# The ring of low weights, and all that is placed behind it, 64 bytes further on

## What is computed

```python
def swiglu(x, w_gu, w_down):
    gate, up = jnp.split(x @ w_gu, 2, axis=-1)
    return (jax.nn.silu(gate) * up) @ w_down
...
for i in range(N_A_LAYERS):
    x = x + 0.5 * swiglu(rms_norm(x, ffn1_norm[l]), ffn1_w_gu[l], ffn1_w_down[l])
    h = rms_norm(x, mix_norm[l]) @ a_w_in[i]
```

## Time and profile before

| | |
|---|---|
| median of 3 runs | 1196.7 us |
| lowest, highest | 1196.52, 1197.67 us |
| profiled execution, first to last instruction | 1195.0 us |
| PE busy | 1187.3 us (99%), 7956 matmuls |
| DVE busy | 934.7 us (78%) |
| ACT busy | 730.4 us (61%) |

### The profile page before, as it was taken

One profiled execution on the slowest core, in us unless ns is written; L12 is line 12 of the kernel. 1 busy time (PEld: TensorE's weight loads), 2 busy tenths in 40 slices (PEclk: granted clock), 3 DMA queues, 4 the chain that ended last, 5 costly groups with the idle time before them and its releaser, 6 DMA issues.

```text
span 1195.0 us, 22393 instructions
## 1 busy us (share of the span) xinstructions
PE 1187.3 (99%) x7956; PEld 1089.4 (91%) x7956; DVE 934.7 (78%) x1617; ACT 730.4 (61%) x1211; POOL 77.9 (7%) x91
## 2 busy tenths in 40 slices
PE   9999999999999999999999999999999999999998
PEld 9899999888888999999888889988888989888887
DVE  7766788988876788688988767888876787888853
ACT  7564746666654588567666645666664567666642
POOL 4460000000000000610000000000000000000000
PEclk9999999999999999999999999999999999999999
DMA  8545655554654445115555743655663423555730
GB/s 329 184 142 187 232 189 177 186 208 176 230 214 154 141 170 188 41 36 177 211 178 204 258 151 123 211 176 194 219 239 135 150 91 125 195 205 178 255 131 36
DMA packets 48143, 209.92 MB, mean 176 GB/s; under 512 B 3486, under 2 KB 4908, under 8 KB 43596
## 3 DMA queue, kind: packets, MB, share of 16 engines
q1 hardware_dynamic: 46720, 204.96, 48.7%
q10 hardware_dynamic: 1356, 4.07, 1.0%
HBM read 207.90 MB, written 1.13 MB: 175 GB/s over the span
## 4 chain that ended last, share of the span: by engine, by line
PE 93%; DVE 4%; ACT 1%; issue 1%; DMA 1%; DVEq 0%; SPq 0%; ACTq 0%
PE main L2165 25%; PE main L2167 13%; PE main L2523 13%; PE main L2138 8%; PE main L2139 8%; PE main L2140 8%; PE main L2525 7%; DVE w_lo L1157 1%; PE side L2303 1%; PE main L2566 1%; PE side L2566 1%; PE side L2277 1%; PE main L2682 1%; PE main L2854 1%; PE main L2858 1%
## 5 line engine op out<-in xcount | busy, mean ns | idle before, releaser
L1157 DVE TENSOR_TENSOR w_lo<-raw,w_hi 128x1024 fp32r<-128x1024 f32 (+3 forms) x365 | 466.8, 1287 | 5.0 <-ACT w_hi L594 3.8
L2165 PE MATMUL main<-xs,w_hi 128*128 128x512 f32 x1328 | 461.3, 390 | 0.2 <-DVE xs L1191 0.2
L594 ACT ACTIVATE w_hi<-raw 128x1024 fp32r<-128x1024 f32 (+2 forms) x363 | 402.5, 1111 | 68.3 <-PE main L2140 53.0
L2167 PE MATMUL main<-xs,w_lo 128*128 128x256 f32 x1328 | 374.5, 282 | 0.0
L2165 PEld LDWEIGHTS main<-xs,w_hi 128*128 128x128 f32 x1328 | 249.2, 188 | 53.2 <-DVE w_lo L1157 0.7
L2167 PEld LDWEIGHTS main<-xs,w_lo 128*128 128x128 f32 x1328 | 251.0, 189 | 0.0
L2523 PE MATMUL main<-h_both,w_hi 128*128 128x512 f32 x682 | 236.6, 390 | 0.0
L2525 PE MATMUL main<-h_both,w_lo 128*128 128x256 f32 x682 | 192.3, 282 | 0.0
L2523 PEld LDWEIGHTS main<-h_both,w_hi 128*128 128x128 f32 x682 | 128.0, 188 | 26.8
L2525 PEld LDWEIGHTS main<-h_both,w_lo 128*128 128x128 f32 x682 | 128.9, 189 | 0.0
L2138 PE MATMUL main<-xs,w_hi 128*128 128x256 f32 x368 | 105.4, 286 | 0.0
(11 more groups left out here) (505 smaller groups left out, 1869.6 us busy)
## 6 DMA issues: line engine op xcount, KB each, us to landing
raw<-in_w_gu_a SPq DMA_DIRECT2D x44, 1024.0 KB, 5.2
raw<-in_w_gu_b SPq DMA_DIRECT2D x44, 1024.0 KB, 5.2
raw<-in_w_down_a SPq DMA_DIRECT2D x16, 1408.0 KB, 6.1
raw<-in_w_down_b SPq DMA_DIRECT2D x16, 1408.0 KB, 6.0
raw<-in_w_in SPq DMA_DIRECT2D x15, 1024.0 KB, 5.4
raw<-in_w_in_a SPq DMA_DIRECT2D x13, 1024.0 KB, 5.2
raw<-in_w_gates SPq DMA_DIRECT2D x4, 1024.0 KB, 5.1
raw<-in_w_up SPq DMA_DIRECT2D x4, 1024.0 KB, 5.2
```

Source lines behind the costliest of these rows:

```text
L594: act.activation(w_hi[:, u % RING, 0:n], raw[:, s % RAW, u % 2, 0:n], ACT.Copy).then_inc(hi_ready, 1)
L1157: return dve.tensor_tensor(dst, src, hi.bitcast(F32), ALU.subtract)
L2165: pe.matmul(bank[:, :], piece(w_hi, u, k), xs[:, k], start=k == 0, stop=k == KC - 1, skip_group_check=True)
L2167: ins = pe.matmul(bank[:, 0:SEQ], piece(w_lo, u, k), xs_hi[:, k], start=False, stop=k == KC - 1, skip_group_check=True)
```

## The change

`w_lo` is placed 64 bytes behind the end of `w_hi` instead of directly behind it, so everything placed after it moves by 64 bytes as well. Behind `h_both` another 96 bytes are left free, so that what is placed after it moves by 160: `gate_n`, `gate_s`, `hid`, `xk_hi`, `xk_lo`, `k_nope`, `k_rope`, `v_mla`, `v_pad_b`, `final`. The views `xs` and `h_both` become one view for each stage, taken from a table of offsets; all offsets in the tables equal the places of before (32 and 0), so nothing is changed by that. No instruction, wait, or transfer is added, removed or moved.

```diff
+XS_AT = {"out1": 32, "ffn_a1": 32, "mix_a": 32, "ffn_a2": 32, "ffn_b1": 32, "mix_b": 32, "ffn_b2": 32}
+H_AT = {"a1": 0, "a2": 0, "b1": 0, "b2": 0}
...
+        def placed(name, at, n):
+
+            e = at % 32 // 4
+            return nc.alloc_sbuf_tensor_at(name, [P, e + n], F32R, offset=at - 4 * e)[:, e:e + n]
+
         x, at = place("x", (nc.sbuf_base + 31) // 32 * 32, [P, KC, SEQ])
-        xs, _ = place("xs", at + 32, [P, KC, 2, SEQ], F32R)
-        xs_hi, xs_lo = xs[:, :, 0], xs[:, :, 1]
+        xs_of = {name: placed("xs_" + name, at + off, KC * 2 * SEQ).rearrange("p (k i n) -> p k i n", k=KC, i=2)
+                 for name, off in XS_AT.items()}
...
         w_hi, at = place("w_hi", at, [P, RING, UNIT], F32R)
-        w_lo, at = place("w_lo", at, [P, RING, UNIT], F32R)
+        w_lo, at = place("w_lo", at + 64, [P, RING, UNIT], F32R)
...
-        h_both, at = place("h_both", free0, [P, 2, FT, SEQ], F32R)
-        h_hi, h_lo = h_both[:, 0], h_both[:, 1]
+        h_of = {name: placed("h_" + name, free0 + off, 2 * FT * SEQ).rearrange("p (i k n) -> p i k n", i=2, k=FT)
+                for name, off in H_AT.items()}
+        at = free0 + 4 * 2 * FT * SEQ + 96
```

More of the change, by code:

```diff
@@ L782, in residual @@
                 if name != "end2":
-                    scale_hi(xs_hi[:, row, :], x[:, row, :], gain("ffn_b1" if name == "kv" else name, row))
+                    split = "ffn_b1" if name == "kv" else name
+                    scale_hi(xs_hi_of[split][:, row, :], x[:, row, :], gain(split, row))
                 square(x[:, row, :], SEQ, c + m)
@@ L823, in up @@
                     act.wait_ge(hid_ready, f * FT + t + 1 + i * 4)
-                    act.activation(h_hi[:, row, :], hid[:, t % 2, :], ACT.Copy).then_inc(h_hi_ready, 1)
+                    act.activation(h_of[which][:, 0, row, :], hid[:, t % 2, :], ACT.Copy).then_inc(h_hi_ready, 1)
                 turns = (FT - first - 2) // 4
@@ L1050, in _ @@
                 act.wait_ge(hid_ready, f * FT + t + 1)
-                act.activation(h_hi[:, t, :], hid[:, t, :], ACT.Copy).then_inc(h_hi_ready, 1)
+                act.activation(h_of["b1"][:, 0, t, :], hid[:, t, :], ACT.Copy).then_inc(h_hi_ready, 1)
                 if t == 0:
@@ L1494, in residual @@
                     dve.wait_ge(evac, t + m + 1 + off)
-                    scale_lo(xs_lo[:, row, :], xm, gain(split, row), xs_hi[:, row, :],
+                    scale_lo(xs_lo_of[split][:, row, :], xm, gain(split, row), xs_hi_of[split][:, row, :],
                              XG0[split] + m, off)
@@ L1552, in hidden @@
                     dve.wait_ge(h_hi_ready, n + 1 + b)
-                    low(h_lo[:, tt, :], hid[:, t % 2, :], h_hi[:, tt, :]).then_inc(h_ready, 1)
+                    low(h_of[which][:, 1, tt, :], hid[:, t % 2, :], h_of[which][:, 0, tt, :]).then_inc(h_ready, 1)
                 turns = (FT - first - 2) // 4
@@ L1846, in _ @@
                 dve.wait_ge(h_hi_ready, f * FT + t + 1)
-                low(h_lo[:, t, :], hid[:, t, :], h_hi[:, t, :]).then_inc(h_ready, 1)
+                low(h_of["b1"][:, 1, t, :], hid[:, t, :], h_of["b1"][:, 0, t, :]).then_inc(h_ready, 1)
                 if t == 0:
@@ L2157, in project, with project_halves @@
                 unit_end(ins)
-            def project_halves(u, bank, off=0, first=None):
+            def project_halves(u, bank, xs, off=0, first=None):
                 unit_begin(u, off)
@@ L2166, in project_halves @@
                               skip_group_check=True)
-                    ins = pe.matmul(bank[:, 0:SEQ], piece(w_lo, u, k), xs_hi[:, k], start=False, stop=k == KC - 1,
+                    ins = pe.matmul(bank[:, 0:SEQ], piece(w_lo, u, k), xs[:, k, 0], start=False, stop=k == KC - 1,
                                     skip_group_check=True)
@@ L2491, in ffn @@
                 f, u0, t0 = FFNS.index(which), first_unit("w_gu_" + which), FIRST_TILE["gu_" + which]
+                xs, h_both = xs_of[FFN_NORM[which]], h_of[which]
                 def turn(i, first=None):
                     if first is not None and which != "a1":
-                        enter(u0, [bank_of(t0 + j) for j in range(2)], (xs_hi, xs_lo) if which == "b2" else (xs,), first,
+                        enter(u0, [bank_of(t0 + j) for j in range(2)], (xs[:, :, 0], xs[:, :, 1]) if which == "b2" else (xs,), first,
                               2 if which == "b2" else 1, None if which == "b2" else FFN_NORM[which])
@@ L2498, in turn @@
                         if which == "b2" and first is not None:
[L2499 removed]
+                            project(u0 + j, bank_of(t0 + j)[:, 0:SEQ], xs[:, :, 0], xs[:, :, 1],
                                     within=(KC - 2, lambda: norm_sum(FFN_NORM[which])) if j == 2 else None)
                         else:
[L2502 removed]
+                            project_halves(u0 + j, bank_of(t0 + j, i * 4), xs, i * 4, first if j == 0 else None)
                         if first is not None and which == "a1" and j == 0:
@@ L2524, in down @@
                                           stop=k == FT - 1, skip_group_check=True)
-                                ins = pe.matmul(bank[:, 0:SEQ], piece(w_lo, u, b), h_hi[:, k, :], start=False,
+                                ins = pe.matmul(bank[:, 0:SEQ], piece(w_lo, u, b), h_both[:, 0, k, :], start=False,
                                                 stop=k == FT - 1, skip_group_check=True)
```

40 lines of the change are left out of this document (22 added, 18 removed).

## The result

The changed kernel takes 1203.96 us, the median of three runs (1203.65 to 1205.06), against 1196.7 before: a ratio of 1.006, 95% interval 1.0042 to 1.0078. It is slower, by 7.3 us. The profiled execution spans 1202.1 us, 7.1 more than the 1195.0 of before.

A forecast was written before the change was run, and what follows sets the result against it. PE, busy 99% of the 1195.0 us span, was taken as the bound. Long matmuls (5.1 us) and short ones (0.7 us) added 5.8 us, giving 1200.8, plus an unchanged 1.7 us around the span: 1202.5 us, range 1188.0 to 1206.5.

The forecast's parts named there:

- The rule that carried it: Likeliest case, slower, chance 0.41: minus 32 is a worse distance than 32 for weights loaded beside the long matmul.
- The long matmuls of the `xs` pairs: 512-column matmuls beside low-weight loads: 1344 at 3.8 ns more each, 5.1 us, the pair going to 350.5 ns.
- The changed short loads: Short matmuls beside a load at a changed distance, in `h_both` pairs and triples: 1814 at 0.4 ns, 0.7 us.
- the choice of the smallest reading: Pricing short matmuls at 0.4 ns, the smallest direct reading at 256 columns, since mixed distances seemed to cost little.
- the small projection: Matmuls passing through eight distances, 117.9 ns on average as on `xs`; taken as evidence against a strong dependence on distance.
- The prices of the 272-column rows: `xg` read from its first token, at minus 32 before the change: 1.1 to 3.3 ns more per matmul.
- The 160 bytes of `xk`: Moved `xk_hi` and `xk_lo`, 72 matmuls: at most 0.7 us at 10 ns each, as likely nothing; only in the range.
- The rival "same": Distance makes no difference or repeats every 64 bytes, so the time stays at 1196.7 us; chance 0.28.
- The rule quoted from the Trainium skill: PE has two independent read ports, so loading weights takes no read bandwidth from the running matmul; time would stay 1196.7 us.
- The rival "faster": Unequal distances to high and low weights break an unlucky rhythm of stream and load: 5 to 8 us gained, 1190 us; chance 0.31.

The follow-up runs named there:

- e1: Changed kernel with the low-weight ring put back directly behind the high one, views by stage and 96 bytes behind `h_both` kept: 1196.78 us.
- e2: Changed kernel with the low-weight ring in its old place and everything behind it still 64 bytes further on: 1200.81 us.
- e7: Changed kernel with `acc` and everything behind it 192 bytes further on, so all tokens are at 32 from high and 224 from low weights: 1204.53 us.
- e11: Changed kernel with low weights directly behind high ones and everything in SBUF, tokens included, 64 bytes further on: 1196.98 us.
- e3: Changed kernel with low weights, and everything behind them, moved by 128 bytes instead of 64: 1199.62 us.
- e6: Changed kernel with other offsets of `xs` and `h_both` in each feed-forward part, low weights still 64 bytes on: 1204.88 us in one execution.
- e12: Changed kernel run again unedited, in five more executions and with a new profile: 1203.97 us.

## Why the prediction was right, and where its steps were off

*Direction and size.* 1202.5 us was forecast, 1203.96 measured, in a range of 1188.0 to 1206.5. The rule that carried it, a distance of minus 32 costs more than one of 32 for the low weights loaded beside the long matmul, is what e1, e2, e7 and e11 show. That the sum came within 1.5 us is in part luck: one term was too high and the other far too low.

*The long matmuls of the `xs` pairs*, 3.8 ns and 5.1 us, measured 4.4 us, 3.3 ns on average over 1328. The forecast was one rate of 350.5 ns; there are two, 348.9 and 353.3, whose mean is near by luck. The price, too, was weaker than it looks: 2.56 us over 11 starts, from rows given to 10 ns, leaves it open by 0.9 ns either way. In b2 the short matmul got longer too (120.6 ns on average against 118.3), which the forecast excluded. So the term is about right and the picture behind it too simple.

*The changed short loads*, 0.4 ns on 1814 matmuls, 0.7 us: off in its parts. In the `h_both` pairs it was 0.0, as the page shows. In triples behind the rings it was 2.2 ns on average, 5 times my price, and over all three matmuls of a triple, not the two with a changed load. `xg` lost 1.0 to 1.1 ns on average, and not where the forecast put it: between 98 and 119 us the first matmul of a triple, the one with the changed load beside it, stayed at 116.0 ns, and the second and third went from 117.0 to 119.2 and 118.1. Together 2.7 us instead of 0.7. The step that failed is the choice of the smallest reading because of the small projection: its 117.9 ns is an average over distances, in which good and bad ones cancel, and it says little on any one of them. The prices of the 272-column rows, 1.1 to 3.3 ns, were the better guide.

*The 160 bytes of `xk`* are next to nothing, as allowed for: at 192/128 its 72 matmuls take 118.1 ns on average, against 117.2 before, 0.1 us.

*The rival "same"* rested on a period of 64 bytes or none. The shift by 64 is the whole effect (e1), and a shift by 128 still shows (e3). The rule quoted from the Trainium skill, "TensorE: Matmul & The Clock Gate", section "Step-by-step: what each phase is for", does not hold for these operands: with the same instructions and clock, where the loaded blocks lie relative to the tokens changes the time by 2.2 or 6.7 ns a pair in the kernel after, and moving both together changes nothing (e11), so loading is not free for the running matmul. What the two streams meet in, no run here shows.

*The rival "faster"* needed a pair below 346.7 ns. For this change it is out: every stage of the kernel after is at 346.7 or above. As an idea it is not. It said that unequal distances can win back part of the 26.7 ns of excess, and at 64/0 in e6 a pair ran at 340.0 ns, an excess of 20.0, until a stall. Even an equal distance, 192/192, gave `xk` triples of 113.7 ns in e2. An estimate from these rows: all 2010 pairs at 340.0 instead of 346.7 would be 13 us less. No run here holds that rate for a stage, and what the rest of the excess is stays open.

*What stays open:* why the same distances allow two rates, and which property of the entry picks one; whether 340.0 ns can be kept for a whole stage; and why b2 is so often the stage that is slower. No version tried beats the kernel before as a whole.

## What to carry to other kernels

Where PE is busy all the time and each matmul has its own weight load, measure the distance between matmul starts to a tenth of a nanosecond, by two far rows of the timeline, before and after any edit that moves a buffer: here 64 bytes in a `place` call cost 0.6%, and no busy share, wait or count showed it, only busy times and lengths. Keep the distance between streaming rows and loaded blocks, modulo 256 bytes, when a layout is changed; a padding in front of all of it is free, as is one of 256 bytes between them, but not one of 64 or 128. An average over mixed distances is no price for one of them. And read the first microseconds of a stage as well as its middle: here the one rate of pairs that beats the kernel before stood only there.

## What the runs showed of the hardware

- The rate of float32r matmuls depends on the distance between the streaming row and the blocks loaded meanwhile, 340.0 to 353.3 ns for a pair of 512 and 256 columns. It repeats at 256 bytes (1196.94 us against 1196.75) and not at 128 (1199.62). Moving everything together changes nothing (1196.98).
- Over whole stages the rates are few: 346.7, 348.9, 350.0 (350.2 in e2), 351.1 and 353.3 ns. At 32/224 both 348.9 and 353.3 hold for whole stages. The same program took either in the same stretch (353.3 in the kernel after, 348.9 in e12, 218 to 225 us), and the rate can change at a stall.
- At 64/0 a pair took 340.0 ns for 25 pairs in e6, and 350.0 behind the next stall. At 32/32 it took 346.7 in every stage read.
- DVE's load made no difference at 32/32: in the kernel before, 346.7 ns beside 85% and 62% of DVE. At the distances with two rates this is not shown.
